# Regrouping the projection matmuls between the state steps: two slots of four triples in place of three slots

## The reference, cut to what matters

```python
p = xn @ w_in                              # 1024 -> 3*512 + 1824 columns
gB, gC, hA = split(p[..., :1536])          # "conv" columns
y_a = gC * causal_dwconv(gB * hA, conv_a_w)
r, k, v, wd, ad, gd = split(token_shifted(p[..., 1536:]))
def step(S, inp):                          # one of 512 tokens, 8 heads of 64 x 64
    sa = einsum('bhvk,bhk->bhv', S, -kk_t)
    S = S * w_t + sa (x) (kk_t * a_t) + v_t (x) k_t
    return S, einsum('bhvk,bhk->bhv', S, r_t)
y_b = (head_group_norm(y) + bonus) * g
out = concat([y_a, y_b]) @ w_out
```

## Time and profile before

| what | value |
|---|---|
| time, median of 3 runs | 1894.42 us (1893.68, 1894.42, 1898.27) |
| the profiled execution's own time | 1897.38 us |
| its span | 1895.6 us |
| mean granted clock of PE | 0.998 |
| PE busy | 1869.7 us (99% of the span) |
| DVE, ACT busy | 1153.5 us (61%), 742.7 us (39%) |
| chain that ended last, by engine | PE 97%, DVE 1%, ACT 1%, issue 1% |

### The profile page before, as it was taken

One profiled execution on the slowest core, in us unless ns is written; L12 is line 12 of the kernel. 1 busy time (PEld: TensorE's weight loads), 2 busy tenths in 40 slices (PEclk: granted clock), 3 DMA queues, 4 the chain that ended last, 5 costly groups with the idle time before them and its releaser, 6 DMA issues.

```text
span 1895.6 us, 28420 instructions
## 1 busy us (share of the span) xinstructions
PE 1869.7 (99%) x11745; PEld 1511.0 (80%) x11745; DVE 1153.5 (61%) x1707; ACT 742.7 (39%) x1074; POOL 30.3 (2%) x72
## 2 busy tenths in 40 slices
PE   7998999999999999999999999999999999999999
PEld 5687778988888888787777788888787777778887
DVE  5864567776763373467687845455446687864534
ACT  5623435322222355333543344335523444334421
POOL 3000000000000000000000000000000000000000
PEclk9999999999999999999999999999999999999999
DMA  4220115233332421222222222252122222222232
GB/s 151 89 68 26 46 47 178 67 97 104 89 105 95 150 66 64 86 70 78 67 78 89 79 69 88 78 160 85 45 90 89 67 62 94 89 67 67 71 108 89
DMA packets 163965, 161.53 MB, mean 85 GB/s; under 512 B 13877, under 2 KB 146267, under 8 KB 163835
## 3 DMA queue, kind: packets, MB, share of 16 engines
q1 hardware_dynamic: 163136, 158.99, 27.0%
q10 hardware_dynamic: 698, 0.71, 0.1%
HBM read 157.59 MB, written 2.10 MB: 84 GB/s over the span
## 4 chain that ended last, share of the span: by engine, by line
PE 97%; DVE 1%; ACT 1%; issue 1%; DMA 0%; ACTq 0%; DVEq 0%
PE psum L637 76%; PE psum L2126 6%; PE psum L2672 2%; PE psum L627 2%; PE psum L2649 1%; PE psum L2629 1%; PE psum L2657 1%; PE psum L573 1%; PE psum L1011 1%; PE psum L1026 1%; PE psum L1040 1%; PE psum L582 0%; PE psum L2754 0%; PE psum L765 0%; DMA param_rows<-in_conv_a_w_dram 0%
## 5 line engine op out<-in xcount | busy, mean ns | idle before, releaser
L637 PE MATMUL psum<-h_hi,w_hi 128*128 128x512 f32 x1376 | 548.9, 399 | 0.9 <-DVE y_feats L1822 0.7
L637 PE MATMUL psum<-h_hi,w_lo 128*128 128x512 f32 x1376 | 536.6, 390 | 0.0
L637 PE MATMUL psum<-h_lo,w_hi 128*128 128x512 f32 x1376 | 536.5, 390 | 0.0
L425 DVE TENSOR_TENSOR w_lo<-w_raw,w_hi 128x2048 fp32r<-128x2048 f32 (+1 forms) x135 | 283.9, 2103 | 277.8 <-ACT w_hi L2861 265.0
L637 PEld LDWEIGHTS psum<-h_hi,w_hi 128*128 128x128 f32 x1376 | 258.6, 188 | 74.3 <-issue 15.7
L637 PEld LDWEIGHTS psum<-h_hi,w_lo 128*128 128x128 f32 x1376 | 258.5, 188 | 54.6
L637 PEld LDWEIGHTS psum<-h_lo,w_hi 128*128 128x128 f32 x1376 | 258.8, 188 | 51.9 <-issue 0.2
L2861 ACT ACTIVATE w_hi<-w_raw 128x2048 fp32r<-128x2048 f32 (+1 forms) x98 | 167.2, 1706 | 251.0 <-PE psum L637 246.4
L637 PE MATMUL psum<-w_hi,h_hi 128*128 128x512 f32 (+1 forms) x448 | 171.4, 383 | 0.1
L637 PE MATMUL psum<-w_lo,h_hi 128*128 128x512 f32 (+1 forms) x448 | 167.8, 375 | 0.0
L637 PE MATMUL psum<-w_hi,h_lo 128*128 128x512 f32 (+1 forms) x448 | 167.7, 374 | 0.0
(11 more groups left out here) (387 smaller groups left out, 2538.1 us busy)
## 6 DMA issues: line engine op xcount, KB each, us to landing
w_raw<-in_w_in_dram SPq DMA_DIRECT2D x162, 512.0 KB, 4.6
w_raw<-in_w_up_dram SPq DMA_DIRECT2D x40, 512.0 KB, 5.2
w_raw<-in_w_out_dram SPq DMA_DIRECT2D x24, 512.0 KB, 4.3
w_raw<-in_w_br_dram SPq DMA_DIRECT2D x48, 256.0 KB, 2.9
w_raw<-in_w_down_dram SPq DMA_DIRECT2D x22, 512.0 KB, 4.3
first_raw<-in_w_in_dram SPq DMA_DIRECT2D x8, 512.0 KB, 7.6
x_first<-in_x_dram SPq DMA_DIRECT2D x4, 512.0 KB, 5.4
up_raw<-in_w_up_dram SPq DMA_DIRECT2D x4, 512.0 KB, 7.8
```

The costliest lines, as they stand in the source:

```text
L425: eng.eng.tensor_tensor(m.wl[:, g % 2, 0:n], m.raw[:, g % 2, 0:n], m.wh[:, g % 2, 0:n].bitcast(F32), ALU.subtract).then_inc(eng.done, 1)
L637: last = pe.eng.matmul(out, a(k), b(k), start=(opens and k == 0 and i == 0), stop=(k == kt - 1 and i == 2), skip_group_check=ks is not None)
```

## The change

It drops slot (s, 0) of every step, makes slots (s, 1) and (s, 2) four triples each, puts one more triple in each of ("i", 0), ("i", 1), ("i", 2) and ("i", 3), and moves the parts of the y norm and of the gating to the slots that are left. A step then holds one half of a panel.

```diff
-FILL = [("i", 0, 3), ("i", 1, 3), ("i", 2, 2), *(("x", l, 2) for l in range(1, LEVELS)), ("i", 3, 2)]
-FILL += [(s, f, 2 if (s, f) in ((1, 0), (3, 0), (5, 0)) else 3) for s in range(7) for f in range(3)]
-Y_AT = {(2, 0): ("mean", 0), (2, 1): ("sums", 0), (2, 2): ("split", 0), (3, 0): ("spread", 0),
-        (4, 0): ("mean", 1), (4, 1): ("sums", 1), (4, 2): ("split", 1), (5, 0): ("spread", 1)}
+FILL = [("i", 0, 4), ("i", 1, 4), ("i", 2, 3), *(("x", l, 2) for l in range(1, LEVELS)), ("i", 3, 3)]
+FILL += [(s, f, 4) for s in range(7) for f in (1, 2)]
+Y_AT = {(2, 1): ("mean", 0), (2, 2): ("sums", 0), (3, 1): ("split", 0), (3, 2): ("spread", 0),
+        (4, 1): ("mean", 1), (4, 2): ("sums", 1), (5, 1): ("split", 1), (5, 2): ("spread", 1)}
 LO_AT = ((0, 6), (1, 1), (1, 3), (1, 5))
-GATED_AT = {(0, 0): (0, 1), (0, 1): (2,), (0, 2): (3,)}
+GATED_AT = {(0, 1): (0, 1), (0, 2): (2, 3)}
...
@@ tensor: PE's order @@
                 scores_23(c + 1, TB)
-            fill((s, 0))
             state_sa(s)
             fill((s, 1))
...
@@ scalar: ACT's order @@
-            gates_out((s, 0))
-            y_parts((s, 0))
             state_sa(s)
             y_state(s)
-            hi_halves(panel_ends((s, 0)))
             gates_out((s, 1))
...
-            for f in (0, 2):
-                for j in GATED_AT.get((s, f), ()):
-                    gate_scaled(j)
+            for j in GATED_AT.get((s, 2), ()):
+                gate_scaled(j)
...
@@ vector: DVE's order @@
-            for f in range(2):
-                ready((s, f))
-                from_products((s, f))
-                for j in GATED_AT.get((s, f), ()):
-                    bonus_gated(j)
+            ready((s, 1))
+            from_products((s, 1))
+            for j in GATED_AT.get((s, 1), ()):
+                bonus_gated(j)
             state_next(s)
```

## The result

The changed kernel takes 1902.38 us (median of 5 runs, 1901.69 to 1905.74) against 1894.42 us (5 runs, 1893.24 to 1898.27): a ratio of 1.0037, 95% interval 1.0026 to 1.0048. It is slower by 8 us, just over what a measurement of this kernel can tell; I had forecast 1895.6 us and no change. The profiled execution took 1901.69 us.

What follows compares the result with a forecast made beforehand. PE, busy 99% of the span, was taken to bound the kernel. Against the profiled 1897.38 us: +7.9 - 2.3 - 1.9 - 2.1 - 3.4 = -1.8, so 1895.6 us, range about 1890.5 to 1901.5.

Steps and rivals of the forecast that it cites:

- The solution uncovered: State steps 1, 3, 5, 6: PE waits for DVE before the solution, 2.8, 1.6, 1.9 and 1.55 us; +7.9 us.
- Slots removed: State steps: seven slots go, each saving 0.33 us of switching between small and large matmuls; -2.3 us.
- the y norm: State steps: all four PE waits for parts of the y norm lose their cause; -1.9 us.
- The levels: Inverse: an earlier load of panel 12 shortens PE's instruction-fetch stalls in levels 4 and 3; -2.1 us.
- the rival: Inverse, level 3: the fetch falls behind the load of panel 12, PE stands 4.1 us; 1903.1 us, chance 0.18.
- The clock: Inverse, level 4: PE's clock no longer falls to half speed, as the 3.33 us stall goes; -3.4 us.
- My second rival: State step 1: the clock falls anyway, on the 2.8 us wait, costing 3.4 us; 1899.0 us, chance 0.19.
- the chance of slower: Whole kernel slower: the case of the fetch falling behind the load of panel 12; 1903.1 us, chance 0.18.

Runs made afterwards that it cites:

- e2: The changed kernel with the two gatings of slot (0, 2) moved to slot (1, 1), behind the copy of the right-hand sides: 1898.40 us, ratio 1.0017.
- e5: The changed kernel with slot (s, 0) given back (two triples) in steps 1, 3, 5, 6, and the gatings as in e2: 1894.22 us, ratio 0.9996.
- e7: e1 with the y norm at the changed kernel's places and the gating of e2: 1894.12 us, ratio 0.9997.
- e8: The changed kernel as it is, run again on a second chip as anchor: 1901.31 us, ratio 1.0030.
- e3: The kernel before, with the load of panel 12 started only after the last level of the inverse: 1892.59 us, ratio 0.9985.
- e1: The kernel before with four triples moved ahead and slots of two, three, three triples in every step, y norm and gating unmoved: 1895.34 us, ratio 0.9998.

## Why the prediction was right and where it failed

- **The solution uncovered, +7.9 us.** Right: 7.5 us, by step 2.80, 1.57, 1.84 and 1.32 against 2.8, 1.6, 1.9 and 1.55. Steps 0, 2 and 4 have no wait, as said. e2 takes the queue's part of step 1 away (1.2 us) and leaves what was counted for the banks; e5 shows that two triples, with e2's order of the gatings, cover all four.
- **Slots removed, -2.3 us, and the y norm, -1.9 us.** Right as far as the traces tell. All four waits of the earlier trace rows are gone. The steps of e7 take 76.4 us; with the changed kernel's waits (7.5 for 0.2) and its two clock falls (3.4) that makes 87.1 us, and the changed kernel takes 84.9 (195.3 to 280.2): 2.2 us for seven slots.
- **The levels, -2.1 us.** This step failed. The load came earlier as worked out, and it was the level 3 fetch that decided; but the fetch did not get ahead of it: it came at 157.7 us, 2.7 us into the load. The stalls at L1026 went from 5.9 us to 5.2 us: 0.7 us won, not 2.1. How far a fetch moves with 18 instructions was argued from one spacing, with less than 1 us to spare, and that was no ground for calling it likelier than the rival. The rival's place was right, its price of 4.1 us for the stall too high: it let the fetch wait for the end of the load, the fetch came inside it, and PE stood 2.0 us.
- **The clock, -3.4 us.** This failed twice, and is the larger part of the error. I had it fall only behind a stall of about 3 us. It fell behind 2.01 us in level 3, behind 2.80 in step 1 and behind 1.84 in step 5: 3.4 us not won, and 3.4 us more. A length of stall from which on it falls was the wrong idea altogether, as e2 shows with 2.00 us (no fall) and 1.28 us (a fall) in one execution. My second rival had one such fall in the steps at 3.4 us; there were two at 1.7.
- **Together**, against the profiled execution's own time: +7.5 - 2.3 - 1.9 - 0.7 + 3.4 = +6.0, where +4.3 was measured between the two profiled executions. The rest is ahead of the change: the scores (L969) begin at 128.27 us against 130.10, 1.8 us earlier; the same changed kernel has them at 130.7 in e8, so this is a spread between executions. I had read the two faster runs of the kernel before as runs that kept their clock. In its 62 later runs the mean clock is 0.998 in 37 and 1.000 in only 4, so that they are the exception and the fall in level 4 the rule. Against the median the forecast was +1.2 us, and 8.0 (6.4 in e8) were measured; 1902.38 lies 0.9 us above the range that I gave (1.0037 times 1894.42, 1901.4, is just at its end), and the chance of slower, 0.18, was too small.

The Trainium skill's sentence that PE's store holds 2048 instructions ("Runtime: NRT & Kernel Launch", Instruction fetch mechanics) would leave a late load without effect. e3 won 3.3 us by placing the load later, so this case goes rather with the other sentence there, of two blocks.

## What to carry to other kernels

Before a filler is taken from between two dependent steps, count the whole queue of the engine that must answer, and the PSUM banks that the next step shares with it: it was 1.3 to 2.8 us here though the answer itself takes 0.42. Each further cut of the filler cost about 0.33 us by the traces (too little for the times to show three of them), so put slots only where the trace shows a wait; work that nobody waits for belongs behind the answer in its queue. And a stall of about 2 us cost another 1.7 or 3.4 us in clock in some executions, and nothing in others.

## What was not expected of the hardware

- The clock falls to half behind some stalls and not behind others of the same length. The 2.0 us of level 3 were followed by a fall of 3.4 us in the changed kernel and in e1, of 1.7 us in e8, and by none in e2, where 1.28 us in level 4 were. In the steps it fell behind 2.80 us in all three profiles that have that wait, behind 1.84 us in one of four, and behind 1.57 us in none of the four that have it.
- PE's instruction fetch suffers from a weight load beside it: with a 1 MB load beside a level, PE stood 3.33 and 2.01 us in the groups of 128 small matmuls, without it 1.23 and 0.36. One such load placed 21 us later was worth 3.3 us by the medians, more than e5 won by its places for the slots and the norm (0.7 us).
